# Two key heads' attention items joined on the two halves of the TensorE array

## The reference

```
s = einsum('bgrtd,bgnd->bgrtn', q, k_cmp) * scale            # branch 0: 31 compressed keys
p_cmp = softmax(where(cvalid, s, NEG)) * any_valid
o_cmp = einsum('bgrtn,bgnd->bgrtd', p_cmp, v_cmp)
...                                                          # branch 1: selected key blocks
...                                                          # branch 2: a window of 512 keys
o = gates[..., 0:1] * o_cmp + gates[..., 1:2] * o_slc + gates[..., 2:3] * o_win
```

## Time and profile before

| | |
|---|---|
| median of 3 runs | 3148.64 us (3146.46 to 3150.63) |
| profiled execution | 3151.16 us |
| its span, first to last instruction | 3149.3 us |
| TensorE busy with matmuls | 2975.5 us, 94% |
| TensorE weight loads (beside the matmuls) | 2053.1 us, 65% |
| VectorE busy | 1561.0 us, 50% |
| ScalarE busy | 643.6 us, 20% |
| GpSimd busy | 149.6 us, 5% |
| mean granted TensorE clock | 0.934 of full |

### The profile page before, as it was taken

The page is one execution under the profiler, slowest core; times in us unless marked ns, Lnnn a source line. Parts: engine busy times, 40 slices in busy tenths (PEclk is TensorE's granted clock), DMA queues, the critical chain, the costliest instruction groups (busy, mean ns, idle before and its releaser), DMA issues. The chain is left out here.

```text
span 3149.3 us, 29504 instructions
## 1 busy us (share of the span) xinstructions
PE 2975.5 (94%) x11724; PEld 2053.1 (65%) x11724; DVE 1561.0 (50%) x2776; ACT 643.6 (20%) x1124; POOL 149.6 (5%) x118
## 2 busy tenths in 40 slices
PE   6999999889999999999899999979998999999999
PEld 5666666648888854444346888854454555488888
DVE  3555565537777520222116776646564333366652
ACT  1112211112111010111102111024535222122200
POOL 0000000001000010000001000001230000000000
PEclk9998999899999999999899999989998555999999
DMA  7112111122443321211122444320113000122221
GB/s 291 37 58 89 67 54 54 54 80 107 164 176 125 138 90 54 84 57 57 53 80 80 167 178 146 128 90 30 68 54 134 1 1 1 54 81 80 91 92 46
DMA packets 24488, 274.96 MB, mean 87 GB/s; under 512 B 3480, under 2 KB 4376, under 8 KB 7072
## 3 DMA queue, kind: packets, MB, share of 16 engines
q1 hardware_dynamic: 19440, 266.45, 22.8%
q10 hardware_dynamic: 4912, 6.63, 0.6%
HBM read 270.97 MB, written 2.10 MB: 87 GB/s over the span
## 5 line engine op out<-in xcount | busy, mean ns | idle before, releaser
L323 PE MATMUL bank<-HT,ring 128*128 128x256 f32 x1056 | 257.7, 389 | 20.1 <-ACT HT L671 12.7
L939 PE MATMUL bank<-HT,ring 128*128 128x512 f32 x512 | 261.0, 640 | 0.0
L323 PE MATMUL bank<-arena 128*128 128x256 f32 x1056 | 249.5, 379 | 0.0
L323 PE MATMUL bank<-arena,ring 128*128 128x256 f32 x1056 | 249.5, 379 | 0.0
L323 PEld LDWEIGHTS bank<-HT,ring 128*128 128x128 f32 x1056 | 204.1, 195 | 51.7 <-issue 23.3
L323 PEld LDWEIGHTS bank<-arena 128*128 128x128 f32 x1056 | 200.6, 190 | 27.3
L323 PEld LDWEIGHTS bank<-arena,ring 128*128 128x128 f32 x1056 | 200.6, 190 | 27.3
L400 PE MATMUL bank<-arena,ring 128*128 128x256 f32 x936 | 207.5, 380 | 5.5 <-ACT arena L470 3.9
L267 PE MATMUL bank<-arena,ring 128*128 128x512 f32 x448 | 198.2, 602 | 10.3 <-issue 7.9
L400 PEld LDWEIGHTS bank<-arena,ring 128*128 128x128 f32 x936 | 177.0, 190 | 30.9 <-ACT arena L470 5.1
L244 DVE SCALAR_TENSOR_TENSOR arena<-ring,evec,arena 128x512 f32<-128x512 f32 x224 | 167.3, 747 | 3.8
(11 more groups left out here) (395 smaller groups left out, 4203.8 us busy)
## 6 DMA issues: line engine op xcount, KB each, us to landing
ring<-w_ada SPq DMA_DIRECT2D x33, 2048.0 KB, 8.0
ring<-w_up SPq DMA_DIRECT2D x33, 2048.0 KB, 7.8
ring<-w_down SPq DMA_DIRECT2D x24, 1408.0 KB, 6.0
ring<-w_gdn SPq DMA_DIRECT2D x8, 2048.0 KB, 12.4
ring<-w_ret_qk SPq DMA_DIRECT2D x4, 2048.0 KB, 8.0
ring<-w_ret_v SPq DMA_DIRECT2D x4, 2048.0 KB, 7.9
ring<-w_ret_g SPq DMA_DIRECT2D x4, 2048.0 KB, 7.8
ring<-w_ret_out SPq DMA_DIRECT2D x4, 2048.0 KB, 7.9
```

The costliest lines, as they stand in the source:

```text
L323: last = nc.tensor.matmul(out_, w[:, k, :], x[:, k, :], start=(first and k == 0), stop=(k == 3), skip_group_check=not first)
L939: last = nc.tensor.matmul(B[u % 2][:, :], w[:, u, k, :], HT[:, k, :], start=(k == 0), stop=(k == KC - 1))
```

## The change

The two key heads' items are joined. `ITEMS` loses g: 36 items (r, b, i), and each step does both heads.
- `scores(n)` issues the matmul of g = 0 (rows 0 to 63 of the array) and then of g = 1 (rows 64 to 127), into two separate banks: (0, 1) for even n, (6, 7) for odd n. For b = 0 the eight matmuls alternate between the heads. It waits for the exp of item n - 2 (before: n - 4).
- TensorE's order is `scores(n + 2)`, transposes of g = 0 into bank 2, transposes of g = 1 into bank 3, `values(n - 1)`. Each set of transposes waits for its own scaled probabilities and for the copy of the item before.
- `values(n)` alternates between the heads, g = 0 into the lower half of bank 4, g = 1 into the upper half of bank 5. These banks are used for every r, so the b = 0 item of an r waits for the copy `dve_o` of the one before.
- ScalarE and VectorE do each operation twice, once for each head, except one reciprocal for both; `dve_o` becomes two copies of 64 partitions.
- `Pn`, `PTn` are twice as large, and `KCMP`, `VCMP` move behind them.

```
-        SB = (0, 1, 6, 7)
+        SB = ((0, 1), (6, 7))
...
             def scores(n):
-                if n >= 4:
-                    pe.wait_ge(act_done, at("act", "nsa", "exp", n - 4))
+                if n >= 2:
+                    pe.wait_ge(act_done, at("act", "nsa", "exp", n - 2, 1))
...
-                    last = nc.tensor.matmul(B[SB[n % 4]][:, 0:(i + 1) * P], NX[half(g), r, i * P:(i + 1) * P],
-                                            NX[half(g), 5 + b, 0:(i + 1) * P], start=True, stop=True)
+                    for g in range(NG):
+                        last = nc.tensor.matmul(B[SB[n % 2][g]][:, 0:(i + 1) * P], NX[half(g), r, i * P:(i + 1) * P],
+                                                NX[half(g), 5 + b, 0:(i + 1) * P], start=True, stop=True)
...
             def values(n):
                 if b == 0:
-                    if g == 0 and r >= 2:
-                        pe.wait_ge(dve_done, at("dve", "nsa", "o", r - 2))
+                    if r:
+                        pe.wait_ge(dve_done, at("dve", "nsa", "o", r - 1))
...
                     for j in range(i + 1):
-                        last = nc.tensor.matmul(O[half(g), i * P:(i + 1) * P], VSW[:, j, (b - 1) * P + g * ND:(b - 1) * P + (g + 1) * ND],
-                                                tiles(PTn[n % 2])[:, j, :], start=False, stop=True, skip_group_check=True)
+                        for g in range(NG):
+                            last = nc.tensor.matmul(B[4 + g][half(g), i * P:(i + 1) * P], VSW[:, j, (b - 1) * P + g * ND:(b - 1) * P + (g + 1) * ND],
+                                                    PTn[n % 2][:, g, j * P:(j + 1) * P], start=False, stop=True, skip_group_check=True)
...
-            for n, (r, g, b, i) in enumerate(ITEMS):
-                if n + 3 < len(ITEMS):
-                    scores(n + 3)
-                pe.wait_ge(dve_done, at("dve", "nsa", "p", n))
-                if n >= 2:
-                    pe.wait_ge(act_done, at("act", "nsa", "pt", n - 2))
-                p4 = tiles(Pn[n % 3])
-                for j in range(NT if b == 0 else i + 1):
-                    last = nc.tensor.transpose(B4[2 + n % 2][:, j, :], p4[:, j, :], ident[:, :])
-                last.then_inc(pe_done, PE.tick("nsa", "pt", n))
+            for n, (r, b, i) in enumerate(ITEMS):
+                if n + 2 < len(ITEMS):
+                    scores(n + 2)
+                for g in range(NG):
+                    pe.wait_ge(dve_done, at("dve", "nsa", "p", n, g))
+                    if n:
+                        pe.wait_ge(act_done, at("act", "nsa", "pt", n - 1, g))
+                    for j in range(NT if b == 0 else i + 1):
+                        last = nc.tensor.transpose(B4[2 + g][:, j, :], Pn[n % 3][:, 4 * g + j, :], ident[:, :])
+                    last.then_inc(pe_done, PE.tick("nsa", "pt", n, g))
                 if n:
                     values(n - 1)
...
-            nc.vector.tensor_copy(HT[:, 4 + r, :], B[4 + r % 2][:, :]).then_inc(dve_done, DV.tick("nsa", "o", r))
+            nc.vector.tensor_copy(HT[half(0), 4 + r, :], B[4][half(0), :])
+            nc.vector.tensor_copy(HT[half(1), 4 + r, :], B[5][half(1), :]).then_inc(dve_done, DV.tick("nsa", "o", r))
```

More of the change, by code:

```diff
@@ L1865, in program @@
         assert o <= 4 * HH * T
-        o = work + 6 * T
+        o = work
+        Pn = [region(o + m * 2 * T, 2 * NT, P) for m in range(3)]; o += 6 * T
+        PTn = [region(o + m * 2 * T, 2, T) for m in range(2)]; o += 4 * T
+        tri = region(o, T); o += T
         KCMP = region(o, 32); o += 32
         VCMP = region(o, 2, ND); o += 2 * ND
[L1869 to L1872, removed]
-        SB = (0, 1, 6, 7)
+        assert o <= 26000
+        SB = ((0, 1), (6, 7))
         NORMED = [4, 0, 1, 2, 3, 6, 7]
@@ L1876, in program @@
         SCALE = ND ** -0.5
-        ITEMS = [(r, g, b, i) for r in range(4) for g in range(NG) for b, i in [(0, 0)] + [(b, i) for b in (1, 2) for i in range(NT)]]
+        ITEMS = [(r, b, i) for r in range(4) for b, i in [(0, 0)] + [(b, i) for b in (1, 2) for i in range(NT)]]
         def half(g):
@@ L1941, in scores @@
                 last.then_inc(pe_done, PE.tick("nsa", "score", n))
             def values(n):
-                r, g, b, i = ITEMS[n]
-                pe.wait_ge(act_done, at("act", "nsa", "pt", n))
-                O = B[4 + r % 2]
+                r, b, i = ITEMS[n]
+                pe.wait_ge(act_done, at("act", "nsa", "pt", n, 1))
                 if b == 0:
-                    if g == 0 and r >= 2:
-                        pe.wait_ge(dve_done, at("dve", "nsa", "o", r - 2))
-                    last = nc.tensor.matmul(O[half(g), :], VCMP[0:NCMP, g, :], PTn[n % 2][0:NCMP, :], start=True, stop=True)
+                    if r:
+                        pe.wait_ge(dve_done, at("dve", "nsa", "o", r - 1))
+                    for g in range(NG):
+                        last = nc.tensor.matmul(B[4 + g][half(g), :], VCMP[0:NCMP, g, :], PTn[n % 2][0:NCMP, g, :], start=True, stop=True)
@@ L1996, in exp @@
             def exp(n):
-                r, g, b, i = ITEMS[n]
-                act.wait_ge(dve_done, at("dve", "nsa", "max", n))
+                r, b, i = ITEMS[n]
                 if n >= 3:
-                    act.wait_ge(pe_done, at("pe", "nsa", "pt", n - 3))
+                    act.wait_ge(pe_done, at("pe", "nsa", "pt", n - 3, 1))
                 if b == 0:
-                    ins = nc.scalar.activation(tiles(Pn[n % 3])[:, :, 0:NCMP], B4[SB[n % 4]][:, :, 0:NCMP], ACT.Exp, scale=SCALE)
-                else:
-                    ins = nc.scalar.activation(Pn[n % 3][:, 0:(i + 1) * P], B[SB[n % 4]][:, 0:(i + 1) * P], ACT.Exp, scale=-1.0,
-                                               bias=small[:, 20 + n % 3:21 + n % 3], accum_out=small[:, 40 + n % 3:41 + n % 3])
@@ L2006, in exp @@
-                ins.then_inc(act_done, AC.tick("nsa", "exp", n))
+                    for g in range(NG):
+                        act.wait_ge(dve_done, at("dve", "nsa", "max", n, g))
+                        nc.scalar.activation(Pn[n % 3][:, 4 * g:4 * g + 4, 0:NCMP], B4[SB[n % 2][g]][:, :, 0:NCMP], ACT.Exp, scale=SCALE)\
+                            .then_inc(act_done, AC.tick("nsa", "exp", n, g))
+                else:
+                    for g in range(NG):
+                        act.wait_ge(dve_done, at("dve", "nsa", "max", n, g))
+                        c = 2 * (n % 2) + g
+                        nc.scalar.activation(Pn[n % 3][:, 4 * g:4 * g + i + 1, :].rearrange("p j c -> p (j c)"), B[SB[n % 2][g]][:, 0:(i + 1) * P],
+                                             ACT.Exp, scale=-1.0, bias=small[:, 20 + c:21 + c], accum_out=small[:, 40 + c:41 + c])\
+                            .then_inc(act_done, AC.tick("nsa", "exp", n, g))
@@ L2008, in act_nsa @@
             exp(0)
-            for n, (r, g, b, i) in enumerate(ITEMS):
+            for n, (r, b, i) in enumerate(ITEMS):
                 if n + 1 < len(ITEMS):
                     exp(n + 1)
-                act.wait_ge(pe_done, at("pe", "nsa", "pt", n))
                 if n >= 2:
                     act.wait_ge(pe_done, at("pe", "nsa", "pv", n - 2))
[L2015 to L2019, removed]
+                for g in range(NG):
+                    act.wait_ge(pe_done, at("pe", "nsa", "pt", n, g))
+                    if b == 0:
+                        ins = nc.scalar.activation(PTn[n % 2][0:NCMP, g, :], B[2 + g][0:NCMP, :], ACT.Copy)
+                    else:
+                        ins = nc.scalar.activation(PTn[n % 2][:, g, 0:(i + 1) * P], B[2 + g][:, 0:(i + 1) * P], ACT.Copy)
+                    ins.then_inc(act_done, AC.tick("nsa", "pt", n, g))
@@ L2052, in dve_nsa @@
             for m in range(3):
[L2054 removed]
+                nc.vector.memset(Pn[m][:, :, :], 0.0).then_inc(dve_done, DV.tick())
             nc.vector.memset(tri, 0.0).then_inc(dve_done, DV.tick())
@@ L2058, in dve_nsa @@
             cm = cmask[:, :, 0:NCMP]
+            valid = cmask[:, :, 31:32].rearrange("p i o -> p (i o)")
             def front(n):
-                r, g, b, i = ITEMS[n]
+                r, b, i = ITEMS[n]
                 dve.wait_ge(pe_done, at("pe", "nsa", "score", n))
-                if n >= 3:
-                    dve.wait_ge(act_done, at("act", "nsa", "exp", n - 3))
                 if b == 0:
[L2067 to L2071, removed]
-                else:
[L2073 to L2076, removed]
@@ new lines, in front @@
+                    S = [B4[SB[n % 2][g]][:, :, 0:NCMP] for g in range(NG)]
+                    m4 = [small[:, 24 + 4 * g:28 + 4 * g] for g in range(NG)]
+                    for g in range(NG):
+                        ins = nc.vector.tensor_tensor(S[g], S[g], cm, ALU.add)
+                    step(ins)
+                    for g in range(NG):
+                        ins = nc.vector.reduce_max(m4[g], S[g], AX)
+                    step(ins)
+                    for g in range(NG):
```

(15 more changed lines are left out.)

27 lines of the change are left out of this document (23 added, 4 removed).

## The result

The changed kernel takes 3000.71 us (median of 4 runs, 2998.70 to 3001.53) against 3149.64 us of the kernel before in the same session: ratio 0.9527, 95% interval 0.9511 to 0.9544. Forecast were 3040 us in a range of 3005 to 3100. The kernel before doesn't always take the same time: beside halves_apart two of its 13 executions took 3118.6 and 3129.2 us, with a mean clock of 0.945 and 0.940 over the whole kernel, the others 3149.7 to 3159.5 us with 0.931 to 0.934.

The account below looks back on a forecast made before the run. TensorE, at 1.2 GHz nearly throughout, was taken to set the 244.6 us attention loop. Mixing 177 us at low and 105 at high clock gave 129, plus ends of 7 = 136, saving 109: 3040 us, range 3005 to 3100.

Parts of the forecast that it names:

- 3 records plus 0.30: Joined score matmuls: both heads partly overlap, sum 7.6 against 10.9 us, saving 3.3 us for each r and b.
- 2k + 1 records instead of 4k: Joined values, k matmuls per head: partial overlap, sum 5.9 against 10.1 us, saving 4.2 us for each r and b.
- high-clock sum: Attention loop at 2.4 GHz: joined groups 9.9 us for each r and b, 3.9 at b = 0, 95 us in all.
- S: The `scores` matmuls in the attention loop; forecast 4.0 us for each r and b at the high clock.
- V: The `values` matmuls in the attention loop; forecast 2.7 us for each r and b at the high clock.
- T: The transposes in the attention loop; forecast 3.2 us for each r and b at the high clock.
- case 1: Halves overlap, clock high about half the time: loop 129 plus ends 7 = 136 us, 3040 us; chance 0.40.
- case 3: Halves overlap, clock high throughout the loop: 105 + 6 = 111 us, saving 133, 3018 us; chance 0.17.
- VectorE's waits thin TensorE out and pull the clock down: Argument against a loop at the high clock throughout: when the clock is high, TensorE waits for VectorE; no separate size.
- The waits: Two-item look-ahead and single-buffered output banks: +4 us at the ends, up to 1 us each of three times at high clock.
- VectorE's 91 us as a floor near 3005: With full overlap and high clock, VectorE's work in the loop holds the whole time at about 3005 us.
- case 2: Halves overlap, loop's clock stays low: 177 + 7 = 184 us, saving 61, 3090 us; chance 0.20.

Follow-up runs that it names:

- halves_apart: Changed kernel with TensorE's scores, transposes and values done for head 0, then head 1, so halves never stand back to back: 3153.57 us, ratio to the kernel before 1.0009.
- before_rows128: Kernel before, with every score matmul contracting over all 128 rows instead of its head's 64 (different result): 3041.32 us, ratio 0.9642.
- values_by_head: Changed kernel with values issuing all matmuls of head 0, then all of head 1, instead of alternating: 3013.85 us, ratio 0.9555.
- changed_again: The changed kernel itself, unedited, measured once more beside later experiments: 3006.20 us, ratio 0.9534.
- scores_apart: Changed kernel with only the two heads' scores taken apart, each ahead of its head's transposes; values still overlap: 3112.50 us, ratio 0.9869.
- values_apart: Changed kernel with only the two heads' values taken apart, each behind its head's transposes; scores still overlap: 3036.92 us, ratio 0.9632.
- front_ahead: Changed kernel with VectorE's order edited, which only moved the output copy `dve_o` behind the next front: 3016.31 us, ratio 0.9562.
- one_out_bank: Changed kernel with both heads' values in one bank, 4 or 5 by r, and one 128-partition copy instead of two: 3000.39 us, ratio 0.9512.
- no_scaling: Changed kernel without VectorE's scaling pass for b = 1 and 2 (different result); transposes wait for the reciprocal: 3000.03 us, ratio 0.9515.

## Why the prediction was wrong in size, step by step

- *TensorE sets the loop, and its 1.2 GHz clock is why it is slow.* Right. before_rows128 shows it: 112 us with full rows, some 101 of them by the clock.
- *The halves run side by side, also in their weight loads.* Right as a mechanism, mis-sized as a term. "Records start in program order ... so I take 3 records plus 0.30" and "2k + 1 records instead of 4k" failed. Measured are 2 and 2k: a record can start past waiting ones of the other half. The Trainium skill, "TensorE: Matmul & The Clock Gate", Part 3, says both that tiles run concurrently, which holds, and that matmuls start strictly in program order, which values_by_head contradicts (at k = 2, the first matmul of head 1 doesn't wait for the second of head 0). In the high-clock sum S comes to 3.0, V to 2.8 and T to 2.8 us for each r and b, 8.6 instead of 9.9 (S of 128 is taken from its 0.49 us less the 0.07 by which records overlap), and b = 0 to 0.9 + 1.0 + 1.0 instead of 3.9. That is 8 x 8.6 + 4 x 2.9 = 80 us instead of 95: 15 us.
- *The clock rises because T and V stand closer and S uses both halves.* The rise came, but "the clock high for about half of the time" was the failing step and the larger error. It is high for all but some 7 of 95 us (10 in changed_again). The forecast of case 1 mixed the two rates; at the high one throughout, its own numbers gave 111 us (case 3), 25 less than the 136 forecast. The other 16 are the 15 of the groups above and one of waits. scores_apart and values_apart show that what counted was not the density of T and V but first of all the scores: apart, they leave the clock low though V overlaps (0.54); side by side, they bring it up though V is apart (0.88; 0.97 with V's overlap as well).
- *VectorE's waits thin TensorE out and pull the clock down.* Wrong for this kernel: 5.3 us of waits before the transposes, 92% busy, clock 1.00. It comes near where one wait is longer (front_ahead's first 2.2 us, with a fall behind it; none behind its other two) or where few rows follow a wait (values_apart). The fall at the loop's start doesn't belong to the wait of 2.6 us there: it came at 2434.7, before that wait began at 2434.9. What lies ahead of it is a wait of 1.81 us for VectorE before the loop, which the kernel before has as well.
- *The waits.* The b = 0 values waited 1.1 us in three times for `dve_o` (one_out_bank); I had up to 1 us each. The ends cost about what I took: 2.6 us of waiting at the start (1.4 in changed_again, whose first scores ran at the low clock) and a stretch at the low clock, 1.65 us at the end.
- *VectorE's 91 us as a floor near 3005.* Too high: it is busy 76.8 us in the loop, since one reciprocal serves both heads (64 of 0.16 us became 32) and records of successive passes overlap more. TensorE remained the bound (no_scaling).
- *The transposes don't count for the clock* (the Trainium skill, "TensorE: Matmul & The Clock Gate", Part 4, the reason given for case 2). Whether they count no run here shows. That they keep the clock low is refuted: they are as many in before_rows128 and in the changed kernel, at 0.98 and 0.97.

The sum: 149.6 us, of which some 101 are the clock without any overlap (244.6 to 132.6, less the 11 us of smaller fixed parts that only full-height scores have) and some 49 the overlap at the high clock. The split is an estimate; no run has half-height scores apart at the high clock throughout. The other way round, the values' overlap at the low clock is 40 (239.9 to 199.7), and the scores' overlap with the clock that it brings is 105.

## What to carry to other kernels

Where TensorE is busy without a gap and the clock reads 0.5, look for matmuls that use few rows: making them use all rows, or setting two half-height ones side by side, can be worth more by the clock than by the overlap. Here they filled some 40% of TensorE's time; what a smaller share does no run shows. Two halves overlapped fully, fp32's two records and their weight loads included, where no more than four records of one half stood ahead of the other's. Price such a change at both clock levels. If the forecast case takes the half-height groups away, sum it at the level of a full-height stretch (1.00 in the earlier trace rows), not at the mean of the two.

## What the runs showed that I had not expected

- A TensorE with 99% busy time stayed at 1.2 GHz for nearly all of 245 us with 64-row matmuls in some 40% of its time, and ran at 2.4 GHz with the same stream at 128 rows (0.52 against 0.98), though the values' matmuls use 64 columns in both.
- Records of one half start past waiting ones of the other half: full overlap with four ahead, 2.6 and 4.6 records lost with six and eight ahead.
- Column halves may fill one bank side by side at full rate: V of k = 4 takes 1.02 us in one_out_bank as in the changed kernel.
- At 2.4 GHz a 64-row group of 512 columns costs 1.06 us to the next group's start, a 128-row one 0.96: half height costs 0.1 us a group, and 0.05 to 0.06 more at the transposes behind it.
- The profiled executions entered the loop between 2433.5 and 2445.9 us, in code that no edit touched. Differences of a few us are therefore read from the loop and not from the whole time.
